# The last accumulations and the residual addition of a decoder layer, done by DMAs that add in place

## What is computed

```python
    x = x + rms_norm(mix, g_mix_post[layer])          # called x1 in the kernel

    h = rms_norm(x, g_ffn_pre[layer])
    ff = (jax.nn.silu(h @ w_gate[layer]) * (h @ w_up[layer])) @ w_down[layer]
    x = x + rms_norm(ff, g_ffn_post[layer])
```

## Time and profile before

| | us |
|---|---|
| median of 3 runs | 2082.83 (2082.64 to 2082.87) |
| the profiled execution | 2083.53 |
| its span, first to last instruction | 2081.7 |
| PE busy in the span | 1998.4 (96%) |
| VectorE, ACT, GpSimd busy | 1114.0, 684.9, 113.6 |

### The profile page before, as it was taken

How to read it: one execution, slowest core, us unless ns; L and a number is a source line. 1 busy time by engine, 2 the same in 40 slices (tenths; PEclk the granted TensorE clock), 3 DMA queues, 4 the chain that set the end, 5 groups by cost and what they waited for, 6 DMA issues and landing times. The chain is left out here.

```text
span 2081.7 us, 21411 instructions
## 1 busy us (share of the span) xinstructions
PE 1998.4 (96%) x9062; PEld 1651.1 (79%) x9062; DVE 1114.0 (54%) x1278; ACT 684.9 (33%) x850; POOL 113.6 (5%) x64
## 2 busy tenths in 40 slices
PE   8999879999998999999999999999999999999994
PEld 6888667778886888888888888888888788888873
DVE  5753585563225433433334333343334788888887
ACT  5331463453226222222222222222222633333342
POOL 1200130000003000000000000000000000000034
PEclk9999999999998999999999999999999999999997
DMA  7433201115321554454444654445542756545633
GB/s 240 111 101 96 66 12 57 54 43 200 101 94 48 192 162 129 125 168 139 137 144 140 194 144 137 118 135 158 150 134 79 267 222 243 212 181 214 242 124 119
DMA packets 292058, 293.24 MB, mean 141 GB/s; under 512 B 4899, under 2 KB 228220, under 8 KB 286204
## 3 DMA queue, kind: packets, MB, share of 16 engines
q1 hardware_dynamic: 288928, 285.23, 43.1%
q10 hardware_dynamic: 3036, 6.66, 1.0%
HBM read 243.09 MB, written 51.93 MB: 142 GB/s over the span
## 5 line engine op out<-in xcount | busy, mean ns | idle before, releaser
L534 PE MATMUL pair<-act_hi,whi 128*128 128x512 f32 x1712 | 669.7, 391 | 0.0
L536 PE MATMUL pair<-act_hi,wlo 128*128 128x512 f32 x1712 | 666.5, 389 | 0.0
L535 PE MATMUL pair<-act_lo,whi 128*128 128x512 f32 x1712 | 666.3, 389 | 0.0
L425 DVE TENSOR_TENSOR wlo<-raw,whi 128x2048 fp32r<-128x2048 f32 x134 | 296.2, 2213 | 247.5 <-ACT whi L418 247.5
L534 PEld LDWEIGHTS pair<-act_hi,whi 128*128 128x128 f32 x1712 | 321.7, 188 | 67.0 <-issue 1.1
L536 PEld LDWEIGHTS pair<-act_hi,wlo 128*128 128x128 f32 x1712 | 321.5, 188 | 67.1
L535 PEld LDWEIGHTS pair<-act_lo,whi 128*128 128x128 f32 x1712 | 321.7, 188 | 66.1 <-issue 0.5
L418 ACT ACTIVATE whi<-raw 128x2048 fp32r<-128x2048 f32 x135 | 248.5, 1843 | 358.9 <-PE pair L536 338.3
L1979 PE MATMUL pair<-ring_hi,hfs 128*128 128x512 f32 x528 | 206.3, 391 | 4.6 <-DVE ring_lo L1500 4.6
L1981 PE MATMUL pair<-ring_hi,hfs 128*128 128x512 f32 x528 | 206.0, 390 | 0.0
L1980 PE MATMUL pair<-ring_lo,hfs 128*128 128x512 f32 x528 | 206.0, 390 | 0.0
(11 more groups left out here) (260 smaller groups left out, 2125.5 us busy)
## 6 DMA issues: line engine op xcount, KB each, us to landing
raw<-in_w_gate SPq DMA_DIRECT2D x44, 1024.0 KB, 5.5
raw<-in_w_up SPq DMA_DIRECT2D x44, 1024.0 KB, 5.7
w_b<-in_w_down SPq DMA_DIRECT2D x40, 1024.0 KB, 5.0
h_forms<-hst SPq DMA_DIRECT2D x22, 1792.0 KB, 7.3
hfs<-h_forms SPq DMA_DIRECT2D x30, 1024.0 KB, 7.7
raw<-in_w_in SPq DMA_DIRECT2D x19, 1024.0 KB, 5.7
raw<-in_w_o SPq DMA_DIRECT2D x16, 1024.0 KB, 4.9
xin<-in_x SPq DMA_DIRECT2D x4, 1024.0 KB, 11.2
```

The lines of the kernel that those rows point to most:

```text
L425: last = nc.vector.tensor_tensor(dst, src, f(hi), ALU.subtract)
L534: nc.tensor.matmul(out_ap, a[0], b[0], start=first, stop=False)
L535: nc.tensor.matmul(out_ap, a[0], b[1], start=False, stop=False)
L536: return nc.tensor.matmul(out_ap, a[1], b[0], start=False, stop=last)
```

## The change

The two mixing steps and the GpSimd additions are rewritten, in four parts.

- *Accumulators.* `add_into` becomes a DMA issued by GpSimd that adds its source into its destination (`accum_op`). Nothing of it starts before product PRODUCTS - 8 = 76, the last of the iteration before the last, has been added. For cb = 0 seven such DMAs are issued (the two mixes among them), for cb = 1 five. Each chain step waits for the landing of the one before. VectorE keeps the two mixes for cb = 1 alone, in `mix_last`.
- *Order on VectorE and ACT.* The mixes no longer stand in `product_add`; `mix_last` stands behind the `form_lo` of the last product, between gains. ACT's squares of cb = 0 stand behind its `form_hi` of the last product.
- *Output.* x1 is stored to the output tensor itself, not to `x1_dram`, and isn't read back. After the scaling, eight DMAs issued by GpSimd add the eight half rows (128 x 1024, 512 KB) into the output in place.
- *Scaling.* ACT scales both halves of tiles 0 and 1 and the right half of tile 3; VectorE those of tile 2 and the left half of tile 3 (`y_normed`). GpSimd does no arithmetic there.

The diff, cut to its core:

```diff
-                        sp_.dma_start(x1_dram[t], x1[:, t, :]).then_inc(x1_out, 16)
+                        sp_.dma_start(out_v[t], x1[:, t, :]).then_inc(x1_out, 16)
...
-                elif it + 1 == ITERS and f_ in (1, 3, 4, 5):
-                    sp_.wait_ge(d_lo, n + 1)
-                    t = (1, 3, 4, 5).index(f_)
-                    sp_.dma_start(x1_row[t][:, :], x1_dram[t]).then_inc(x1_in[t], 16)
...
-            def add_into(dst, src, cb):
-                a, b = y[dst][:, :, 512 * cb:512 * cb + 512], y[src][:, :, 512 * cb:512 * cb + 512]
-                nc.gpsimd.tensor_tensor(a, a, b, ALU.add).then_inc(y_based, 1)
...
+            def add_into(dst, src, cb, done):
+                a, b = (y[m][:, :, 512 * cb:512 * cb + 512] for m in (dst, src))
+                nc.gpsimd.dma_start(a, b, accum_op=ALU.add).then_inc(done, 16)
+
+            pool.wait_ge(*evictions(PRODUCTS - 8))
+            add_into(5, 0, 0, u_in_y5)
+            add_into(2, 0, 0, u_in_y2)
+            pool.wait_ge(u_in_y2, 16)
+            add_into(1, 2, 0, u_in_y1)
+            add_into(6, 2, 0, u_in_y6)
+            pool.wait_ge(u_in_y1, 16)
+            add_into(4, 1, 0, u_in_y4)
+            pool.wait_ge(u_in_y6, 16)
+            add_into(6, 3, 0, y3_in_y6)
+            pool.wait_ge(y3_in_y6, 16)
+            add_into(3, 1, 0, y1_in_y3)
...
+            def add_to_out(t, half):
+                nc.gpsimd.dma_start(out_v[t][:, 1024 * half:1024 * half + 1024], y_part(t, half),
+                                    accum_op=ALU.add).then_inc(y_out, 16)
...
+                if n == PRODUCTS - 1:
+                    act.wait_ge(d_done, PRODUCTS - 7)
+                    for half, t0, done in ((0, 0, u_in_y5), (1, 0, u_in_y4), (0, 2, y3_in_y6), (1, 2, y1_in_y3)):
+                        act.wait_ge(done, 16)
+                        y_square(t0, half, 0)
+                        y_square(t0 + 1, half, 0)
...
+                if n == PRODUCTS - 3:
+                    dve.wait_ge(u_in_y4, 32)
+                elif n == PRODUCTS - 2:
+                    dve.wait_ge(u_in_y5, 32)
...
+            def mix_last():
+
+                dve.wait_ge(u_in_y6, 32)
+                dve.wait_ge(u_in_y1, 32)
+                dve.wait_ge(*evictions(PRODUCTS - 4))
+                nc.vector.tensor_tensor(y_of(6, 1), y_of(6, 1), y_of(3, 1), ALU.add).then_inc(y_mixed, 1)
+                dve.wait_ge(y_mixed, 1)
+                nc.vector.tensor_tensor(y_of(3, 1), y_of(3, 1), y_of(1, 1), ALU.add).then_inc(y_mixed, 1)
```

More of the change, by code:

```diff
@@ L302, in build @@
         x1_out = sem("x1_out")
-        x1_in = [sem(f"x1_in{t}") for t in range(TB)]
-        y_based = sem("y_based")
+        u_in_y5, u_in_y2, u_in_y1, u_in_y4, u_in_y6, y3_in_y6, y1_in_y3 = (
+            sem(n) for n in ("u_in_y5", "u_in_y2", "u_in_y1", "u_in_y4", "u_in_y6", "y3_in_y6", "y1_in_y3"))
         y_mixed = sem("y_mixed")
@@ L648, in _ @@
                     fetch_h(done // 14 + 1, done % 7)
[L650 to L658, removed]
+            sp_.wait_ge(y_out, 16 * 2 * TB)
         @block.gpsimd
@@ new lines, in _ @@
+            add_into(5, 0, 1, u_in_y5)
+            pool.wait_ge(*evictions(PRODUCTS - 5))
+            add_into(2, 0, 1, u_in_y2)
+            pool.wait_ge(u_in_y2, 32)
+            add_into(1, 2, 1, u_in_y1)
+            add_into(6, 2, 1, u_in_y6)
+            pool.wait_ge(u_in_y1, 32)
+            pool.wait_ge(u_in_y4, 16)
+            add_into(4, 1, 1, u_in_y4)
+            def add_to_out(t, half):
+                nc.gpsimd.dma_start(out_v[t][:, 1024 * half:1024 * half + 1024], y_part(t, half),
+                                    accum_op=ALU.add).then_inc(y_out, 16)
@@ L748, in _ @@
+            pool.wait_ge(x1_out, 16 * TB)
+            for t in (0, 1):
+                for half in (0, 1):
+                    pool.wait_ge(y_scaled, 2 * t + half + 1)
+                    add_to_out(t, half)
+            for half in (0, 1):
+                pool.wait_ge(y_ready, half + 1)
+                add_to_out(2, half)
+            pool.wait_ge(y_scaled, 5)
+            add_to_out(3, 1)
+            pool.wait_ge(y_ready, 3)
+            add_to_out(3, 0)
         @block.scalar
@@ L1083, in _ @@
                     product_copy(m)
[L1084 to L1089, removed]
+                if n == PRODUCTS - 1:
[4 more added lines that the diff above has]
+                        y_square(t0 + 1, half, 0)
+                    act.wait_ge(y_mixed, 2)
+                    y_square(2, 1, 1)
+                    y_square(3, 1, 1)
+                if m in (PRODUCTS - 3, PRODUCTS - 2):
                     act.wait_ge(*evictions(m))
-                    half, t0 = ((1, 0), (0, 0), (0, 2))[m % 7 - 4]
-                    y_square(t0, half, cb)
-                    y_square(t0 + 1, half, cb)
+                    y_square(0, PRODUCTS - 2 - m, 1)
+                    y_square(1, PRODUCTS - 2 - m, 1)
             def root_of(t0, t1, n):
@@ L1097, in root_of, with y_times_rstd @@
                 nc.scalar.activation(root[:, t0:t1], mean[:, t0:t1], ACT.Sqrt).then_inc(root_done, 1)
-            def y_times_rstd(t):
-                a = y_part(t, 1)[:, shared(t)]
-                nc.scalar.activation(a, a, ACT.Copy, scale=rstd[:, t:t + 1]).then_inc(y_scaled, 1)
+            def y_times_rstd(t, half):
+                nc.scalar.activation(y_part(t, half), y_part(t, half), ACT.Copy,
+                                     scale=rstd[:, t:t + 1]).then_inc(y_scaled, 1)
             root_of(0, 2, 8)
@@ L1106, in _ @@
             act.wait_ge(rstd_ready, 4)
-            act.wait_ge(gained, 6)
-            y_times_rstd(0)
-            y_times_rstd(1)
+            act.wait_ge(gained, 7)
+            y_times_rstd(0, 0)
+            y_times_rstd(0, 1)
             root_of(2, 3, 9)
@@ L1599, in y_rstd, with y_normed @@
                 dve.wait_ge(rstd_ready, n_rstd)
[L1601 to L1610, removed]
+            def y_normed(t, half):
+                nc.vector.tensor_scalar(y_part(t, half), y_part(t, half), rstd[:, t:t + 1], None,
+                                        ALU.mult).then_inc(y_ready, 1)
             def late_piece(t):
                 dve.wait_ge(d_first if t == 2 else d_done, 1 if t == 2 else PRODUCTS)
-                dve.wait_ge(y_mixed, 3)
+                dve.wait_ge(y_mixed, 1)
                 a = y[6][:, t - 2, 512:1024]
@@ L1631, in _ @@
             dve.wait_ge(gained, 8)
-            y_residual(2)
+            y_normed(2, 0)
+            y_normed(2, 1)
             y_rstd(3, 4, 16, 10, 6, lambda: late_gain(3))
             dve.wait_ge(gained, 9)
-            y_residual(3)
+            y_normed(3, 0)
         @block.tensor
```

49 lines of the change are left out of this document (11 added, 38 removed).

## The result

The changed kernel takes 2120.93 us (median of 5 runs, 2118.08 to 2123.18), the kernel before beside it 2082.83: a ratio of 1.0182, 95% interval 1.0167 to 1.0196. The forecast was 2087.6 us with a range of 2066 to 2112. The side was right, though the forecast lay hardly beyond what it called no change; the size was not right: the profiled span is 2121.4 us where the sum gave 2086.5, 34.9 us more.

The account below looks back on a forecast made before the run. Bound: VectorE's chain behind GpSimd's additions, then, after the change, the DMA additions. Sum: 2007.5 + 6 s' + 12 d + 14.5 + 0.3 = 2086.5 of span; plus 1.83 less 0.70 gives 2087.6 us, range 2066 to 2112.

Parts of the forecast that it names:

- Bound and gaps of TensorE: Last 100 us: no TensorE gap over 1 us, no half-clock stretch before, TensorE done near 2044; DMA additions end last.
- the 11.3 us: TensorE's losses near the end: gaps of 3.7 and 4.1 us, slower matmuls 1.7 and 1.8 us; expected off the path.
- s and d: Per in-place DMA addition: s, turn to landing with nothing ahead, 5.0 us; d, time taking up the engines, 2.6 us.
- two additions go out together and the second is waited for: s' + d: Accumulator chain after product 76's eviction at 2007.5: first two additions overlap, the second (y0 into y2) being waited for.
- s': One in-place DMA addition from its issue on GpSimd to landing: s of 5.0 plus 0.5 for issue, 5.5 us.
- a smaller way: Accumulator chain: each in-place addition waits until the one before has drained; 14.5 us at most.
- the dearer stretch of 2096 to 2125: Outcome range for the last rivals, such as all three passes counting (s' 6.8, d 3.9, 2111 us); chance 0.25.
- From the mix to the first row: Tail: mixes, gains, additions, reduction, inverse root, late piece, then ACT's square and scaling until the first row is written; 14.5 us.
- s' + 7 d + 0.3: End of kernel: eight output additions follow one another at d after the first scaling, plus 0.3 us to the end.
- GpSimd's hold on VectorE in the tail: Tail: stretching of VectorE by GpSimd goes, 1.9 us each on two L1147 and L1622, about 1 on last L1608.
- Small operations stretched while GpSimd issues DMAs: Sign of being wrong another way: VectorE's small operations still stretched, now by GpSimd writing descriptors.
- The rival "as cheap as a copy": In-place additions cost s 2.6, d 1.3; mix at 2033.6, end 2063.5 us; with its half way point, chance 0.33.

Follow-up runs that it names:

- plain: The changed kernel with the 12 DMAs between y buffers copying instead of adding, 1024 bytes of descriptor space, accumulator sums left out; 2085.38 us (one run).
- tail_dve: The kernel before, with VectorE adding both halves of every row, without GpSimd's additions into the rows and ACT's scalings; 2077.42 us, ratio 0.9975.

## Why the prediction was wrong, point by point

- **Bound and gaps of TensorE: right.** No hole, full clock (1.00), last matmul at 2043.11 (forecast: done at 2044.1). That the 11.3 us would be off the path was right too, since the kernel ends 78 us behind it.
- **s and d: right.** 5.0 and about 2.75 us, for 5.0 and 2.6, and 2.5 us an addition into the output; the addition costs the engines twice a copy (2.80 against 1.29 us in plain). The issue on GpSimd is 1.2 us for an addition between buffers, not 0.5, but it lies mostly beside the landing.
- **The step that failed: "two additions go out together and the second is waited for: s' + d".** They don't. The space of 1024 bytes holds one such addition, so each takes its whole 5.3 us or more. I had this as "a smaller way", 14.5 us at most and in the accumulator chain alone. There it is 15.4 us. But it was not the smaller way, it was the case; and it holds for the output too, where I let eight DMAs follow one another at d: three fit, and the wait costs another 10.15 us. Together 25.5 of the 34.9 us by the two profiles (22.0 by the medians). Its true price on the sum, 25.5 us for 14.5, would have put that rival at 2113, just past the end of the range. What came out, 2120.93, lies in the dearer stretch of 2096 to 2125 that the prediction gave a chance of 0.25.
- **A row left out, and a collision that was too cheap.** With space for all, the chain took 45.7 us instead of the sum's 40.5. The first pair, beside the 1 MB of g_row, took 11.6 us instead of 8.1, 3.5 more, where I wrote 2.6 at most. I also left y1 into y4 out of the chain of cb = 0, where it stands ahead of y3 into y6; with space for all its cost was small (5.89 us to that landing for 5.5), but in the changed kernel it is one more addition in the line, 11 up to the mix (61.05 / 11 = 5.55 us each) where the prediction counted ten. The three in a row took 12.0 for 10.7.
- **From the mix to the first row: nearly right.** 14.5 us forecast, 15.66 measured (2068.24 to 2083.90), of which 0.5 are a wait of VectorE for a DMA.
- **The output at the end: the same step.** s' + 7 d + 0.3 gave 24.0 us; with 2048 bytes it is 27.35, with 1024 it is 37.5. The price of one was right: seven in a row go at 2.5 us each. But also 2048 bytes are too little for eight. The last one starts when the others have landed and takes 6.15 us where 2.5 and the way to the end were reckoned; by my estimate that is some 3 of the 3.35 us left. No run gave more space, so this part is not shown.
- The sum over again, against 2086.5: space 15.4 + 10.15, chain 5.2, mix to first row 1.2, the rest of the output 3.35, start −0.3 = 35.0; measured 34.9.
- **GpSimd's hold on VectorE in the tail: right.** In tail_dve, too, the stretched operations are gone, and its tail is 4.1 us shorter although VectorE adds all the rows. **Small operations stretched while GpSimd issues DMAs: refuted**, L1157 takes 0.16 at 2084.63, while GpSimd issues two output DMAs (2083.90 to 2085.70).
- **The rival "as cheap as a copy", 2063.5 us:** its first half (mix at 2033.6) is what plain shows, its end is not, as the output's DMAs went on adding there.
